# Expert loop of a two-block transformer kernel: the one unsplit weight half is split like the other eleven

## What is computed

```python
    top_vals, top_idx = lax.top_k(logits, TOP_K)          # TOP_K = 4 of 32 experts
    gates = jax.nn.softmax(top_vals, axis=-1)
...
    xs = xt[slot_tok].reshape(n_blocks, MOE_BLOCK, d)     # blocks of 128 tokens of one expert

    def expert_block(args):
        xb, e = args
        hgu = xb @ w_up_gate[e] + b_up_gate[e]            # 1024 x 2048
        x_glu = jnp.minimum(hgu[:, :D_EXPERT], SWIGLU_LIMIT)
        x_lin = jnp.clip(hgu[:, D_EXPERT:], -SWIGLU_LIMIT, SWIGLU_LIMIT)
        hact = x_glu * jax.nn.sigmoid(SWIGLU_ALPHA * x_glu) * (x_lin + 1.0)
        return hact @ w_down[e] + b_down[e]               # 1024 x 1024
```

## Time and profile before

| | us |
|---|---|
| median of 3 runs | 2767.11 (2760.39 to 2773.5) |
| the profiled execution's own time | 2767.25 |
| its span, first to last instruction | 2765.1 |
| stretch of the expert loop in which the turns are alike, 1488.87 to 2652.00 | 1163.13 |

### The profile page before, as it was taken

One profiled execution on the slowest core, in us unless ns is written; L12 is line 12 of the kernel. 1 busy time (PEld: TensorE's weight loads), 2 busy tenths in 40 slices (PEclk: granted clock), 3 DMA queues, 4 the chain that ended last, 5 costly groups with the idle time before them and its releaser, 6 DMA issues.

```text
span 2765.1 us, 29671 instructions
## 1 busy us (share of the span) xinstructions
PE 2569.4 (93%) x10025; PEld 1768.3 (64%) x10025; DVE 1673.3 (61%) x2124; ACT 1281.5 (46%) x1489; POOL 143.6 (5%) x99
## 2 busy tenths in 40 slices
PE   5999999899999999685969999999999999999968
PEld 2456564688744444364457777777777778777754
DVE  2223652555400225675468888888888888888842
ACT  2033141433200110960137766676766677776642
POOL 1000000000000000000000110011111011111010
PEclk9995899899999999566969999999999999999989
DMA  8120330223212210021549999999999999999960
GB/s 288 50 91 1 122 107 31 92 92 110 95 54 91 74 61 0 0 84 32 179 148 367 362 361 369 364 368 362 363 362 365 365 365 367 363 362 360 370 221 31
DMA packets 286482, 570.29 MB, mean 206 GB/s; under 512 B 10556, under 2 KB 35031, under 8 KB 286391
## 3 DMA queue, kind: packets, MB, share of 16 engines
q1 hardware_dynamic: 273607, 523.69, 52.5%
q0 software_dynamic: 12816, 45.81, 6.1%
HBM read 542.71 MB, written 26.75 MB: 206 GB/s over the span
## 4 chain that ended last, share of the span: by engine, by line
PE 89%; DVE 5%; ACT 3%; issue 2%; DMA 1%; SPq 0%; DVEq 0%; POOL 0%; ACTq 0%; POOLq 0%
PE bank L1158 15%; PE bank L1441 12%; PE bank L1443 12%; PE bank L1442 12%; PE bank L1318 6%; PE bank L1133 5%; PE bank L1435 4%; PE bank L1306 3%; PE bank L1307 3%; PE bank L1308 3%; PE bank L1197 3%; PE bank L1215 3%; PE bank L1166 2%; PE bank L1505 2%; PE bank L1430 2%
## 5 line engine op out<-in xcount | busy, mean ns | idle before, releaser
L1931 DVE TENSOR_TENSOR w_lo<-stage,w_hi 128x2048 fp32r<-128x2048 f32 x364 | 818.7, 2286 | 73.8 <-ACT w_hi L1051 51.4
L1051 ACT ACTIVATE w_hi<-stage 128x2048 fp32r<-128x2048 f32 x364 | 685.5, 1912 | 229.2 <-PE bank L1443 227.5
L1441 PE MATMUL bank<-w_hi,xeT_hi 128*128 128x512 f32 x1056 | 439.3, 416 | 0.0
L1443 PE MATMUL bank<-w_hi,xeT_lo 128*128 128x512 f32 x1056 | 412.9, 391 | 0.0
L1442 PE MATMUL bank<-w_lo,xeT_hi 128*128 128x512 f32 x1056 | 412.9, 391 | 0.0
L1158 PE MATMUL bank<-ring,hT 128*128 128x512 f32 (+1 forms) x960 | 410.0, 589 | 2.0 <-ACT hT L905 2.0
L1158 PEld LDWEIGHTS bank<-ring,hT 128*128 128x128 f32 x960 | 182.9, 191 | 225.3 <-issue 222.7
L1443 PEld LDWEIGHTS bank<-w_hi,xeT_lo 128*128 128x128 f32 x1056 | 199.2, 189 | 43.0
L1442 PEld LDWEIGHTS bank<-w_lo,xeT_hi 128*128 128x128 f32 x1056 | 199.7, 189 | 40.4
L1441 PEld LDWEIGHTS bank<-w_hi,xeT_hi 128*128 128x128 f32 x1056 | 200.5, 190 | 37.3
L1441 PE MATMUL bank<-w_hi,eaT_hi 128*128 128x512 f32 x400 | 176.0, 440 | 0.0
(11 more groups left out here) (375 smaller groups left out, 3272.2 us busy)
## 6 DMA issues: line engine op xcount, KB each, us to landing
stage<-in_w_up_gate SPq DMA_DIRECT2D x264, 1024.0 KB, 7.4
stage<-in_w_down SPq DMA_DIRECT2D x132, 1024.0 KB, 5.1
ring<-in_w_ada SPq DMA_DIRECT2D x12, 2048.0 KB, 8.6
ring<-in_w_up SPq DMA_DIRECT2D x22, 1024.0 KB, 7.7
ring<-in_w_in SPq DMA_DIRECT2D x10, 2048.0 KB, 7.8
ring<-in_w_out SPq DMA_DIRECT2D x4, 2048.0 KB, 12.5
ring<-in_w_down SPq DMA_DIRECT2D x4, 2048.0 KB, 8.0
stage<-in_w_ple_gate SPq DMA_DIRECT2D x4, 1024.0 KB, 7.1
```

What stands on the lines that cost most here:

```text
L1051: fn(w_hi[top_of(h)][:, :], src[:, :], ACT.Copy).then_inc(s_hi, 1)
L1441: mm(bank[b][:, :], hi[:, kk, :], wh[:, k, :], start=False, stop=False)
L1443: ins = mm(bank[b][:, :], lo[:, kk, :], wh[:, k, :], start=False, stop=kk == KT - 1)
L1931: tt(w_lo[h][:, :], stage[h][:, :], w_hi[top_of(h)][:, :].bitcast(FP), ALU.subtract).then_inc(s_lo, 1)
```

## The change

Half 8 joins the split halves. `SPLIT` now lists all twelve. ACT no longer writes `ea_whole`, but copies a high part of half 8; DVE subtracts one more low part, between those of 7 and 9; PE multiplies half 8 in 12 fp32r matmuls in place of four float32 ones.

```diff
-WHOLE = 8
-SPLIT = [h for h in range(HALVES) if h != WHOLE]
+SPLIT = list(range(HALVES))
...
-    ea_whole = at(R + 68 * KB, [P, KT // 2, P], name="ea_whole")
...
-                    if j == 0 and whole is not None:
-                        fn(whole[:, :, :], blk3(bank[b][:, :]), ACT.Copy)
...
-                tiles_T(eaT, 2 * i + (FU[6] + 1), 3 * i + (FU[7] + 3), ea_whole)
-                split_hi(i, 9)
+                tiles_T(eaT, 2 * i + (FU[6] + 1), 3 * i + (FU[7] + 3))
+                split_hi(i, 8, 9)
...
-                    if whole is not None and h == WHOLE:
-                        wv = half_in(pe, i, h)[:, :].rearrange("p (k n) -> p k n", k=KT // 2)
-                        for k in range(KT // 2):
-                            ins = mm(bank[b][:, :], whole[:, k, :], wv[:, k, :], start=False, stop=False)
-                    else:
-                        pe.wait_ge(s_lo, split_no(i, h))
...
+                    pe.wait_ge(s_lo, split_no(i, h))
...
-                split_lo(i, 6, 7, 9)
+                split_lo(i, 6, 7, 8, 9)
```

More of the change, by code:

```diff
@@ L1034, in _, with tiles_T @@
             norm(3, embedding)
-            def tiles_T(dst, k6, k7, whole=None):
+            def tiles_T(dst, k6, k7):
                 for j, (b, k) in enumerate(((6, k6), (7, k7))):
                     act_e.wait_ge(bank_full[b], k)
-                    if j == 0 and whole is not None:
-                        fn(whole[:, :, :], blk3(bank[b][:, :]), ACT.Copy)
                     fn(dst[0][:, 4 * j:4 * j + 4, :], blk3(bank[b][:, :]), ACT.Copy).then_inc(s_xhi, 1)
@@ L1425, in turn, with fill @@
                     ins.then_inc(bank_full[b], 1)
-            def fill(b, lhs, hot_, bcol, i, h0, whole=None):
+            def fill(b, lhs, hot_, bcol, i, h0):
                 hi, lo = lhs
@@ L1431, in fill @@
                 for h in (h0, h0 + 1):
-                    if whole is not None and h == WHOLE:
-                        wv = half_in(pe, i, h)[:, :].rearrange("p (k n) -> p k n", k=KT // 2)
-                        for k in range(KT // 2):
-                            ins = mm(bank[b][:, :], whole[:, k, :], wv[:, k, :], start=False, stop=False)
-                    else:
-                        pe.wait_ge(s_lo, split_no(i, h))
[L1438 to L1443, removed]
+                    pe.wait_ge(s_lo, split_no(i, h))
+                    wh, wl = (a[:, :].rearrange("p (k n) -> p k n", k=KT // 2) for a in (w_hi[top_of(h)], w_lo[h]))
+                    for k in range(KT // 2):
+                        kk = h % 2 * (KT // 2) + k
+                        mm(bank[b][:, :], hi[:, kk, :], wh[:, k, :], start=False, stop=False)
+                        mm(bank[b][:, :], hi[:, kk, :], wl[:, k, :], start=False, stop=False)
+                        ins = mm(bank[b][:, :], lo[:, kk, :], wh[:, k, :], start=False, stop=kk == KT - 1)
                     ins.then_inc(half_read[h // 2] if h == h0 else bank_full[b], 1)
@@ L1454, in up, with down @@
                 fill(c, xeT, hot[0], c * CW, i, 2 * j)
-            def down(i, at_, h0, k6, k7, whole):
+            def down(i, at_, h0, k6, k7):
                 pe.wait_ge(bank_taken[6], k6)
@@ L1462, in down @@
                     pe.wait_ge(bank_taken[4 + n], TK[4 + n] + i)
-                    fill(4 + n, eaT, hot[1], 2 * D + n * CW, at_, h0 + 2 * n, whole)
+                    fill(4 + n, eaT, hot[1], 2 * D + n * CW, at_, h0 + 2 * n)
             def turn_ea(i, k6, k7):
@@ L1491, in _ @@
                 turn(rows, 2 * i + (TK[6] + 1), 3 * i + (TK[7] + 4))
-                down(i - 1, i, 8, 2 * i + (TK[6] + 1), 3 * i + (TK[7] + 3), ea_whole)
+                down(i - 1, i, 8, 2 * i + (TK[6] + 1), 3 * i + (TK[7] + 3))
             turn_ea(nb - 1, 2 * nb + TK[6], 3 * nb + (TK[7] + 2))
-            down(nb - 1, nb, 0, 2 * nb + (TK[6] + 1), 3 * nb + (TK[7] + 3), None)
+            down(nb - 1, nb, 0, 2 * nb + (TK[6] + 1), 3 * nb + (TK[7] + 3))
             norm(4)
```

## The result

The changed kernel takes 2783.85 us (median of 16 runs) against 2773.53 us for the kernel before on the same chips: a ratio of 1.0041, with an interval of 1.0028 to 1.0053. I had forecast 2747, with 2738 to 2759 as the range. The change makes the kernel 0.4% slower; the time lies 25 us above the range's upper end. The profiled execution took 2778.23 us with a span of 2776.1 us.

A forecast was written before the change was run, and what follows sets the result against it. PE was taken to bound the loop's turn of 37.44 us. From 2767.25 us, 23.0 came off for PE, 1.6 was added for a stall at bank 7 and 1.3 behind the loop: 2747.1 us, range 2738 to 2759.

The forecast's parts named there:

- PE: what goes and what comes: Expert loop: half 8's `fill` falls from 6.42 to 5.70 us, 0.72 us a turn, 23.0 us over 32 turns.
- ACT: Loses copy `ea_whole`, gains a 1.9 us high part hidden in idle time; `eaT_hi` 0.47 us earlier; cost nothing.
- DVE, the delay at `found`: One subtraction adds 2.20 us, net 1.73 us at `found`; PE stalls 0.05 us in 31 turns, 1.6 us.
- The slack at bank 7: Between DVE's copy out of bank 7 and PE's weight load for it: 1.68 us of slack.
- Who waits for that?: Listed what stands behind the new subtraction in DVE's order; `found` was called the tightest.
- Would the delay pile up?: On DVE from turn to turn: no, 1.1 us of idle is left and each turn begins afresh.
- DMA: Same 13.6 MB a turn, rate rising to some 371 GB/s; costed at nothing, with 11 us of reserve.
- Behind the loop: PE's wait for DVE's `hot` grows from 2.4 to 3.7 us; adds 1.3 us, bounds 0 and 2.2.
- The sum: Whole kernel: 2767.25 - 23.0 + 1.6 + 1.3 = 2747.1 us, 0.7% below before.
- The first: Rival: DVE leads at bank 7, the wait at `found` stalling PE 0.2 to 0.52 us a turn; 2756 us, chance 0.17.
- The third rival: DVE bounds the turn if its four idle stretches cannot be absorbed: 39.6 us a turn, 2839 us, chance 0.04.
- over 0.2 us a turn at bank 7: Sign in the changed profile: a PE wait this long at bank 7 would show the forecast wrong.

The follow-up runs named there:

- e1: Changed kernel with the two register loads ahead of `pick` moved up, between low parts 4 and 5 and behind 5: 2750.23 us, ratio 0.9922 to the kernel before.
- e2: Changed kernel without half 8's subtraction; PE takes its high part in place of the low one: 2745.88 us, ratio 0.9905 to the kernel before.
- e6: Changed kernel with `pick`'s register loads moved up and `found` moved ahead of low parts 9 and 10: 2747.64 us, ratio 0.9915 to the kernel before.
- e11: Changed kernel; DVE also waits ahead of low part 4 for ACT's high part 5: 2747.90 us, ratio 0.9915 to the kernel before.
- e12: Changed kernel with only `found` moved ahead of low parts 9 and 10 on DVE: 2751.76 us, ratio 0.9935 to the kernel before.
- e4: Changed kernel without POOL's scatter, a no-operation raising its semaphore instead: 2740.74 us in one run, 1.0% below the kernel before.
- e3: Kernel before, half 8 still unsplit, with one more DVE operation of the subtraction's size between low parts 7 and 9: 2781.27 us, ratio 1.0045.
- e10: Changed kernel with POOL's gather issued ahead of the scatter, near the turn's end: 2770.75 us, ratio 1.0001 to the kernel before.
- e7: Changed kernel with POOL's gather held back until DVE has issued `pick`: 2868.48 us, ratio 1.0347 to the kernel before.
- e5: Control: kernel before with the two register loads ahead of `pick` moved up around low part 5: 2770.86 us, ratio 0.9999.
- e8: Changed kernel; DVE waits between low parts 3 and 4 for a POOL no-operation behind the scatter: 2783.07 us, ratio 1.0033 to the kernel before.

## Why the prediction was wrong, point by point

- **PE: what goes and what comes.** Right. Forecast 0.72 us a turn; e1, e2, e6, e11 and e12 run turns of 36.70 us, 0.74 less than before.
- **ACT.** Right. ACT shows no wait for a load, and `eaT_lo` waits 1.08 us where I had said 1.1.
- **DVE, the delay at `found`.** This is the step that failed. I put the stall at 0.05 us a turn, with 0.52 us as the upper bound; it is 1.10 us. The delay of the subtraction itself was well sized: with normal loads PE does not wait at all (e1, e4). What I got wrong is the 0.80 us ahead of `pick`, which I took over from the kernel before as fixed. They grew by 1.24 us in the mean, since one of the two register loads in them now falls just behind the end of the scatter's issue. I never asked what that gap is made of.
- **The slack at bank 7** was misread as well, by less. The row at 2011.90 in the earlier trace rows holds the fourth and the fifth of eight weight loads that start 0.11 us apart, and the first one into bank 7 is the fifth, at 2012.01. And a load that waits follows `picked` by 0.06 us (2014.16 + 0.18 to 2014.40), not by the 0.13 us read at `hot`, where the row names "issue" and not `hot` as what ended the wait. So the slack was some 1.86 us, not 1.68, and the delay of 1.73 us would have left 0.13 us free. The 1.24 us less these 0.13 are 1.11, the 1.10 us measured.
- **"Who waits for that?"** The list named only instructions behind the subtraction in DVE's order. It left out POOL. The scatter's one wait for DVE, the copy of `idx_out`, was met long before (1983.26 in the kernel before), and yet its issue was held by DVE's activity. I named POOL's DMAs nowhere in the working, though the first of the two rows of low parts whose idle, 1.02 and 1.03 us, I took from the earlier trace rows ends 0.05 us before the scatter is issued.
- **"Would the delay pile up?"** Answered rightly for DVE: it does not, each turn begins afresh. But the same paragraph spends the 1.03 us of idle ahead of low part 4 as free cover. That gap was doing work. It was "idle", and the kernel's speed hung on it.
- **DMA.** Right where it could be seen: 371 GB/s in e1, e2, e6, e11 and e12, the forecast's own number, and no wait of ACT. By the 368 GB/s of the Trainium skill (page "DMA: Bandwidth & Descriptors", section "Where 436 GB/s comes from") a turn would have taken an estimated 37.0 us; the turns of 36.70 us disagree. In the changed kernel the rate is 361 because the turn is longer: the same 13.6 MB in 37.74 us.
- **Behind the loop.** Right: forecast 3.7 us, measured 3.9, from 2.4. Waits of PE in the window from 2640 on:

```profile
PE bank L1426 <- DVE hot L2032: 3.9, 1, 3.9
```

- **The sum.** 2747.1 less the 1.6 us of stall that it held, plus the 31.9 us measured, is 2777.4 us; the profiled execution took 2778.23. One term carries the whole miss of the profiled execution. Of the distance between the forecast and the median of 2783.85, 6 us are not its doing: the kernel before, 2767.11 in the three runs that I started from, has a median of 2773.53 beside the changed one.
- **The rivals.** The first named the right place, bank 7, and the wrong cause: its mechanism by itself costs 0.31 us a turn in e3 and nothing in e1. Its price was capped by one subtraction's length, so it could not reach the result. No rival let POOL's issue or a register load change its length. The third rival, priced at 2839, asked whether each idle stretch is a latency; one of the four is, but it grew, which that rival did not foresee. (Its turn of 39.6 us is 37.44 + 2.2; DVE's 34.6 us with the four stretches of 4.73 are 39.3.) A slower kernel had a chance of 0.05 in all. The check "over 0.2 us a turn at bank 7" was the one that fired.

**What stays open.** That the slow load needs the scatter, and not POOL's work at that moment, is shown by e4 and e10: without the scatter no slow load, with POOL idle still a slow one. By which path the scatter does it no run shows. Over all kernels the slow loads start 0.4 to 1.7 us behind the end of the scatter's issue; those of e11 start 4.8 and 5.6 us behind it, while its rows have not all landed (10.1 us from issue to landing), and are normal. So it can only be the early part of the transfer that hurts. What in DVE's row holds the issue is open too. Every row that did so is made of subtractions with both inputs in SBUF; no run puts another kind of operation there. And no run tells why some issues come through between two subtractions and others wait for the end of the row.

The best versions are e6, e11 and e1 (ratios 0.9915, 0.9915 and 0.9922, not told apart by their intervals), at 2747.64 to 2750.23 us. Each keeps the change and gives DVE a pause, or keeps its loads out of the scatter's way.

## What to carry to other kernels

Before an engine's idle time is spent as cover, look at what every other engine starts in it, POOL's indirect DMAs above all: the idle may be what they need. A small gap put down to "issue" is not a constant; open it up to the sequencer's own instructions, and ask which of them read memory and what traffic will run beside them after the change. Where a change makes an engine's work unbroken, compare the durations of all engines in the same window, also of those that the edit never touches: POOL's 118 to 250 us was the quickest sign of the cause.

## What the runs showed of the hardware that I had not expected

- The issue of an indirect DMA on POOL is held by an unbroken row of DVE's subtractions: 1.58 us becomes 7.25 us for the scatter, 0.98 us becomes 5.82 (e4) or 9.40 us (e7) for the gather. A pause of 0.36 us is enough to let the scatter through (2.08 us, e3).
- DVE pays nothing at the time: four low parts take 8.88 us beside a held issue, 2.22 us each, and 2.23 us each in the earlier trace rows.
- A register load on DVE takes 0.31 us, and 0.6 to 1.67 us when it starts 0.4 to 1.7 us behind the end of the scatter's issue. That holds behind a short issue too (1.23 us, e5).
- A no-operation on POOL behind an indirect DMA raised its semaphore before that DMA's issue had ended (e8).
- An added wait made the kernel 1.2% faster (e11 against the changed kernel: 0.9915 against 1.0041 of the kernel before).
